# Mixers whose lanes begin at moments from a table, and weight pieces rounded five beats ahead of their product

## What is computed

```python
def first_block(...):                      # l = 0, 1
    h = h + 0.5 * swiglu(rmsnorm(h, ffn1_norm[l]), w_gate, w_up, w_down)   # d_ff = 2816
    z = rmsnorm(h, mix_norm[l]) @ w_in[l]
    y_mla, y_diff = mla_mixer(...), diff_mixer(...)       # causal attention over 256 rows
    y_pool = pool_mixer(...)                              # running means, then a small product
    branches = einsum('bsnc,ncd->bsnd', stack([y_mla, y_diff, y_pool]), w_branch[l])
    h = h + sum(sigmoid(z_gate) * branches) @ w_out[l]
    h = h + 0.5 * swiglu(rmsnorm(h, ffn2_norm[l]), ...)
return rmsnorm(h, final_norm)

def second_block(...):                     # l = 0, 1
    x = x + 0.5 * rms_norm(swiglu_2(rms_norm(x, ...), w_ffn1_in[l], w_ffn1_out[l]), ...)
    proj = rms_norm(x, ln_mix_pre[l]) @ w_in[l]
    y_attn = sliding_window_gqa(...)                      # 8 heads, window 128, sinks
    y_mlstm = mlstm_chunkwise(...)                        # chunks of 64
    y_rwkv = rwkv7_time_mix(...)                          # a recurrence, computed in chunks
    x = x + rms_norm(concat([y_attn, y_mlstm, y_rwkv]) @ w_out[l], ln_mix_post[l])
    x = x + 0.5 * rms_norm(swiglu_2(rms_norm(x, ...), ...), ...)
    gate = sigmoid(rms_norm(x, ln_ple_pre[l]) @ w_ple_gate[l])
    x = x + rms_norm(gate * (p[l] @ w_ple_proj[l]), ln_ple_post[l])
```

## Time and profile before

| | before |
|---|---|
| median of the runs | 2604.29 us |
| profiled execution, device time | 2605.03 us |
| its span (first to last instruction) | 2603.4 us |
| PE, matmul busy | 2420.7 us (93%) |
| PE, weight load busy | 2044.6 us (79%) |
| DVE busy | 1521.4 us (58%) |
| ACT busy | 1250.3 us (48%) |
| POOL busy | 54.2 us (2%) |
| casts (L260), 748 | 779.0 us |
| subtractions (L267), 748 | 905.4 us |

### The profile page before, as it was taken

One profiled execution on the slowest core, in us unless ns is written; L12 is line 12 of the kernel. 1 busy time (PEld: TensorE's weight loads), 2 busy tenths in 40 slices (PEclk: granted clock), 3 DMA queues, 4 the chain that ended last, 5 costly groups with the idle time before them and its releaser, 6 DMA issues.

```text
span 2603.4 us, 33966 instructions
## 1 busy us (share of the span) xinstructions
PE 2420.7 (93%) x13760; PEld 2044.6 (79%) x13760; DVE 1521.4 (58%) x2356; ACT 1250.3 (48%) x2095; POOL 54.2 (2%) x66
## 2 busy tenths in 40 slices
PE   7998889999999879999999978899988997989997
PEld 6888788888888878888878867678877886867885
DVE  4656576655655657665555566665555557466555
ACT  4445344544544535454454453544455444355444
POOL 0000000000000000000000000000000000000000
PEclk9999899999999989999999989889999998979999
DMA  6554234566566423456655633136645553214553
GB/s 237 195 184 145 81 114 135 180 187 187 178 188 188 149 86 116 136 178 186 187 167 187 188 128 99 58 111 196 187 151 177 186 189 96 89 49 163 190 187 111
DMA packets 110748, 400.12 MB, mean 154 GB/s; under 512 B 12288, under 2 KB 12672, under 8 KB 110336
## 3 DMA queue, kind: packets, MB, share of 16 engines
q1 hardware_dynamic: 110592, 397.96, 48.4%
HBM read 396.86 MB, written 1.05 MB: 153 GB/s over the span
## 4 chain that ended last, share of the span: by engine, by line
PE 79%; DVE 12%; ACT 5%; issue 2%; DMA 1%; POOL 0%; SPq 0%; ACTq 0%; DVEq 0%
PE ps L275 71%; DVE wlo L267 4%; ACT whi L260 2%; PE ps L561 2%; PE ps L1724 1%; DVE alo L417 1%; ACT ahi L394 1%; PE ps L1173 1%; PE ps L378 1%; DVE sm L1221 0%; DVE cv L2274 0%; PE ps L1129 0%; PE ps L1138 0%; ACT S L1190 0%; PE ps L1157 0%
## 5 line engine op out<-in xcount | busy, mean ns | idle before, releaser
L267 DVE TENSOR_TENSOR wlo<-raw,whi 128x1024 fp32r<-128x1024 f32 (+1 forms) x748 | 905.4, 1214 | 718.7 <-ACT whi L260 715.7
L260 ACT CAST whi<-raw 128x1024 fp32r<-128x1024 f32 (+1 forms) x748 | 779.0, 1046 | 663.7 <-PE ps L275 658.1
L275 PE MATMUL ps<-whi,ahi 128*128 128x512 f32 (+2 forms) x1632 | 655.9, 402 | 51.1 <-DVE alo L417 43.8
L275 PE MATMUL ps<-whi,alo 128*128 128x512 f32 (+2 forms) x1632 | 640.2, 392 | 0.0
L275 PE MATMUL ps<-wlo,ahi 128*128 128x512 f32 (+2 forms) x1632 | 639.1, 392 | 0.0
L275 PEld LDWEIGHTS ps<-whi,ahi 128*128 128x128 f32 x1632 | 312.0, 191 | 118.9 <-issue 43.9
L275 PEld LDWEIGHTS ps<-whi,alo 128*128 128x128 f32 x1632 | 311.7, 191 | 63.6
L275 PEld LDWEIGHTS ps<-wlo,ahi 128*128 128x128 f32 x1632 | 312.4, 191 | 58.1 <-issue 0.8
L275 PE MATMUL ps<-whi,yhi 128*128 128x512 f32 (+1 forms) x852 | 335.8, 394 | 2.0 <-DVE ylo L773 1.1
L275 PE MATMUL ps<-whi,ylo 128*128 128x512 f32 (+1 forms) x852 | 332.5, 390 | 0.0
L275 PE MATMUL ps<-wlo,yhi 128*128 128x512 f32 (+1 forms) x852 | 332.3, 390 | 0.0
(11 more groups left out here) (362 smaller groups left out, 2211.7 us busy)
## 6 DMA issues: line engine op xcount, KB each, us to landing
raw<-stream SPq DMA_DIRECT2D x718, 512.0 KB, 3.5
raw<-stream SPq DMA_DIRECT2D x16, 388.0 KB, 3.0
bcb<-bcs SPq DMA_DIRECT2D x9, 512.0 KB, 4.6
raw<-stream SPq DMA_DIRECT2D x8, 416.0 KB, 3.2
raw<-stream SPq DMA_DIRECT2D x4, 384.0 KB, 3.4
cst<-consts SPq DMA_DIRECT2D x1, 1260.0 KB, 6.0
msc<-misc SPq DMA_DIRECT2D x1, 1160.0 KB, 5.9
xs<-xin SPq DMA_DIRECT2D x2, 512.0 KB, 4.5
```

The source lines that it names most:

```text
L260: act.do.copy(whi[:, n % NSP, 0:w], raw[:, n % NRAW, 0:w]).then_inc(*rounded(n))
L267: dve.do.tensor_tensor(wlo[:, n % NSP, 0:w], raw[:, n % NRAW, 0:w], whi[:, n % NSP, 0:w].bitcast(F), ALU.subtract).then_inc(*rest(n))
L275: m = pe.do.matmul(o, a, b, start=(first and q == 0), stop=(last and q == n - 1))
```

## The change

Three things change, and no instruction is added or removed but for a few loads of ACT's function tables (35 in both programs; in L2106 two fewer, in L2242 two more).

- Each piece's rounding is placed by its product: `taken[n]` is PE's beat when it takes piece n, and the cast's beat is the later of the slot's beat and `taken[n]` less 5.0. The subtraction stands 0.5 behind. The DMA of piece n stands where piece n-4 is rounded.
- `freed` takes a distance from PE's own beat rather than a beat; `again` and `first_time` are gone.
- In the mixers, `timed` replaces the beats of every lane by those of a table `PLAN`, relative to `org(s)`. The lanes themselves and the order within each are the same. In `pe_unit` a wait for `"mask"` is one for `"T"`, which DVE sends one multiplication later.

```diff
+LEAD = 5.0
+
+PLAN = {
+    "mix1": {
...
+        "act_latent": (27.1, 31.6, 31.9, 36.1, 38.6, 41.7, 42.1, 42.6, 49.5, 49.5, 49.9, 49.9, 49.9),
...
+    "mix2": {
...
+        "dve_jobs2": (65.8, 67.3, 71.9, 73.4, 75.5, 78.3, 80.9, 83.9),
...
+        taken.append(pe.beat)
...
-    def freed(n, beat, by, *key):
-
-        free[n] = (beat, by.name, key)
+    def freed(n, d, by, *key):
+
+        free[n] = (pe.beat + d, by.name, key)
...
+    def round_beat(n):
+
+        return max(slot_beat(n - NSP), now_taken[n] - LEAD)
...
-            yield slot_beat(n - NRAW - NSP) if n >= NRAW else -2.0
+            yield round_beat(n - NRAW) if n >= NRAW else -2.0
...
     def act_weights():
         for n in range(len(pieces)):
-            yield slot_beat(n - NSP)
+            yield round_beat(n)
...
     def dve_weights():
         for n in range(len(pieces)):
-            yield slot_beat(n - NSP) + 0.5
+            yield round_beat(n) + 0.5
...
-    def first_time(s):
...
+    def timed(s, **lanes):
+
+        def one(name, lane):
+            plan = PLAN.get(PARTS[s][0], {}).get(name)
+            for k, beat in enumerate(lane):
+                yield org(s) + plan[k] if plan else beat
+        return [one(name, lane) for name, lane in lanes.items()]
...
-        def again(k, t):
-
-            return max(t, first_time(s + 1) + 1.36 * k - 2.6)
...
-                    freed(held[k][0], again(k, t + 0.68 * (h + k + 1)), dense, s, "held", k)
+                    freed(held[k][0], 0.68, dense, s, "held", k)
...
-                freed(n, t + GU * (r + 1), dense, s, *(("gu", q, 1) if r == 3 else ("g", q, r)))
+                freed(n, GU, dense, s, *(("gu", q, 1) if r == 3 else ("g", q, r)))
...
-            pe.wait_ge(rec_dve, s, 0, "mask", L64_)
+            pe.wait_ge(rec_dve, s, 0, "T")
...
             elif part == "mix1":
-                lanes += [tables_in(act, s), act_project1(s), act_latent(s, l), act_bias1(s), act_jobs1(s), act_back1(s), act_sums1(s),
-                          act_turn1(s, l), act_pool1(s), act_branch1(s)]
+                lanes += timed(s, tables_in=tables_in(act, s), act_project1=act_project1(s), act_latent=act_latent(s, l),
+                               act_bias1=act_bias1(s), act_jobs1=act_jobs1(s), act_back1=act_back1(s), act_sums1=act_sums1(s),
+                               act_turn1=act_turn1(s, l), act_pool1=act_pool1(s), act_branch1=act_branch1(s))
```

More of the change, by code:

```diff
@@ L220, in program @@
     stages = list(enumerate(PARTS))
-    free = {}
-    now_free, pieces = (known["free"], known["order"]) if known else (free, order)
+    free, taken = {}, []
+    now_free, now_taken, pieces = (known["free"], known["taken"], known["order"]) if known else (free, taken, order)
     def width(n):
@@ L510, in down @@
             m.then_inc(*dense(s, "d", j))
-            freed(n, t + GU, dense, s, "d", j)
+            freed(n, GU, dense, s, "d", j)
         t = step_beat(s, 0)
@@ L794, in pe_wide @@
             m.then_inc(*dense(s, *key, r, i))
-        freed(n, t + 2.9, dense, s, *key, r, 1)
+        freed(n, 2.2, dense, s, *key, r, 1)
     def region(at):
@@ L859, in pe_project1 @@
                 if i:
-                    freed(n, t + Z1 + 1.12 * (5 + r), dense, s, "z", r, 1)
+                    freed(n, 1.12, dense, s, "z", r, 1)
         for c in range(8):
@@ L960, in pe_latent @@
             m.then_inc(*front_pe(s, "v", i))
-        freed(n, t + 26, front_pe, s, "v", 1)
+        freed(n, 3.0, front_pe, s, "v", 1)
         for b in range(5):
@@ L2383, in pe_ple @@
             m.then_inc(*dense(s, "p", hf))
-            freed(n, t + 2.72 * (hf + 1), dense, s, "p", hf)
-        freed(n1, t + 5.44, dense, s, "p", 1)
+            freed(n, 2.72, dense, s, "p", hf)
+        freed(n1, 2.72, dense, s, "p", 1)
         def wait_y(k):
@@ L2443, in tensor_program @@
             elif part == "mix1":
-                lanes += [tables_in(pe, s), pe_project1(s, l), pe_latent(s, l), pe_scores1(s), pe_values1(s), pe_turn1(s, l),
-                          pe_pool1(s, l), pe_branch1(s, l), pe_out1(s, l)]
+                lanes += timed(s, tables_in=tables_in(pe, s), pe_project1=pe_project1(s, l), pe_latent=pe_latent(s, l),
+                               pe_scores1=pe_scores1(s), pe_values1=pe_values1(s), pe_turn1=pe_turn1(s, l), pe_pool1=pe_pool1(s,
+                               l), pe_branch1=pe_branch1(s, l), pe_out1=pe_out1(s, l))
             elif part == "mix2":
-                lanes += [pe_project2(s, l), pe_front2(s, l), pe_unit(s, 0), pe_unit(s, 1), pe_state(s), pe_group(s),
-                          pe_rope2(s), pe_scores2(s), pe_values2(s), pe_turn2(s), pe_memory(s, l), pe_out2(s, l)]
+                lanes += timed(s, pe_project2=pe_project2(s, l), pe_front2=pe_front2(s, l), pe_unit0=pe_unit(s, 0),
+                               pe_unit1=pe_unit(s, 1), pe_state=pe_state(s), pe_group=pe_group(s), pe_rope2=pe_rope2(s),
+                               pe_scores2=pe_scores2(s), pe_values2=pe_values2(s), pe_turn2=pe_turn2(s), pe_memory=pe_memory(s, l),
+                               pe_out2=pe_out2(s, l))
             else:
@@ L2513, in pool_program @@
             if part == "mix1":
-                lanes += [pool_latent(s), pool_sums1(s)]
+                lanes += timed(s, pool_latent=pool_latent(s), pool_sums1=pool_sums1(s))
             elif part == "mix2":
-                lanes += [pool_memory(s)]
+                lanes += timed(s, pool_memory=pool_memory(s))
             if part in POST and part != "final":
@@ L2550, in program @@
     sync_program()
-    return {"at": {name: x.at for name, x in signals.items()}, "free": free, "order": order}
+    return {"at": {name: x.at for name, x in signals.items()}, "free": free, "taken": taken, "order": order}
 def make_consts():
```

89 lines of the change are left out of this document (70 added, 19 removed), and 28 rows, old and new, of the table PLAN.

## The result

The changed kernel takes 2525.72 us (median of four runs, 2522.96 to 2525.82) against 2602.42 for the kernel before in the same comparison: a ratio of 0.9707, 95% interval 0.9686 to 0.9728, or some 76 us less.

A forecast was written before the change was run, and what follows sets the result against it. PE was taken as the bound, with gains only from its idle time in the mixers and the clock. The terms -22.1 - 3.6 - 4.0 + 1.0 gave -28.7 us, so 2575.6 us on the median, range 2560 to 2590.

The forecast's parts named there:

- part 5 of the sum: Inside the FFNs: roundings come later at no cost, hidden by PE's work, with 1.24 us left for piece 154.
- Part (1): In the four mixers: roundings leave the path, gaining 22.1 us of a ceiling of 44.7.
- Part (2): In mix1: the table's own moves shorten PE's wait for `pool_f`, 1.8 us each, 3.6 in all, bounds 0 and 14.4.
- Part (3): In mix2: fewer waits shorten the half-clock stretch, 2 us each, 4 in all, bounds 0 and 24.4.
- Rival A: Deeper: the waits taken away bring the clock back, -71.7 us, 2533 us; chance 0.15.
- Part (4): Between stages, around the norms: roundings move off and onto the path, net +1.0 us, bounds -6.6 and +7.6.
- D: Half: norms at stage borders cost +7.6 us and the share in the first part is 20%, 2590 us; chance 0.12.
- C: Nothing: work moved within a DVE-pressed stage comes back as another wait, 2605 us; chance 0.10.
- B: Slower: the cover in the FFNs fails and PE stalls 0.6 us a step, 2623 us; chance 0.13.

The follow-up runs named there:

- The rule alone: Changed kernel with the table PLAN emptied, so every lane has its old beats and only the new rounding rule stays: 2585.69 us, ratio 0.9936.
- that one lane: Changed kernel whose mix1 table keeps only `pe_values1`, PE's lane of the attention's second products, with mix2's table whole: 2554.86 us, ratio 0.9822.

## Why the prediction was wrong

**Direction and bound: right.** The gain was in the mixers, PE's work did not change, and the FFNs' insides kept their length: 16.79 us a step (part 5 of the sum). But the sizes were not as named: 38.5 and 32.0 us in the two mix1 where 7 to 9 each were to be seen, 2.8 and 4.8 in the two mix2 where 6 to 8 were.

**Part (1), roundings: right in sum by luck, wrong in place.** I took 22.1 of a ceiling of 44.7 us, by my shares some 9 in mix1 and 13 in mix2. The rule alone gave 9.4 + 12.6 in mix1, nearly the whole ceiling there (10.4 + 12.7), and -0.9 - 0.3 in mix2, 20.8 together. The share of 40% was one number for two stages that behave in opposite ways. The 3.5 us a mix2 that I called nearly certain did leave their stretch: no rounding stands in the chain between 1565 and 1605 us of the changed kernel, which corresponds, and from the 399th to the 441st product of weights the stage takes 46.4 us in place of 51.1, with the rule alone 48.6. But the rule alone had lost 2.8 us by the 399th, which I had not weighed.

**Part (2), the table: the step that failed.** I took a quarter of one wait, `pool_f`, 3.6 us in all with 14.4 as the bound. It is worth 29.1 and 19.4 us in mix1 (266.1 to 237.0 and 257.9 to 238.5) and 3.7 and 5.1 in mix2. Why: I looked through ACT's and DVE's programs for roundings, and took PE's own order as given. The wait I priced, `pool_f`, fell from 7.2 to 2.0 us. The ones I did not price fell more. What is left in the first mix1:

```profile
PE ps L369 <- DVE alo L511: 3.8, 1, 3.8
PE ps L1424 <- DVE pool_f L1446: 2.0, 2, 1.8
PE ps L1263 <- ACT PT L1291: 0.9, 3, 0.5
PE ps L1263 <- DVE PT L1332: 0.8, 1, 0.8
PE ps L1247 <- DVE ylo L863: 0.5, 1, 0.5
PE ps L369 <- DVE dk L1000: 0.2, 1, 0.2
```

Of the earlier trace rows, the wait for `zc` is gone. Of the waits before that follow, so are 7 of 8.7 us for `PT`, and those for `S`, `dv` and `o_dif` altogether:

```profile
PE ps L1173 <- ACT PT L1201: 4.4, 10, 0.7
PE ps L1173 <- DVE PT L1242: 4.3, 3, 1.7
PE ps L1157 <- DVE S L1231: 3.1, 4, 0.9
PE ps L275 <- ACT dv L900: 2.8, 1, 2.8
PE ps L761 <- DVE o_dif L1274: 2.2, 1, 2.2
```

The bound of the part should have been the whole of PE's idle time in mix1, 28 and 26 us, with the clock on top.

**Part (3), the clock: wrong stage.** I priced the long half-clock stretch in mix2, which stayed: from 1602 to 1633 us of the changed kernel the clock is 0.57.

```profile
1602.00:1633.00 31.00, 30.75 (x110) 23.03 (x110) 18.43 (x44) 17.26 (x36) 1.01 (x1) 0.57 0.21 68
```

Still in front of it is the stretch in which DVE has the chain, 24.90 of 27 us busy:

```profile
1575.00:1602.00 27.00, 23.22 (x120) 17.00 (x118) 24.90 (x50) 17.22 (x36) 0.00 (x0) 0.88 0.13 40
```

In mix1, whose half-clock stretches I left at nothing, 14.2 and 11.0 us of busy time went. Rival A's condition, that the waits go, was met in mix1; in mix2 it was not, where 23.8 and 24.9 of 29.8 us of idle time stayed, and the clock stayed at 0.85 and 0.87. The rule of the Trainium skill quoted in part (3) (TensorE: Matmul & The Clock Gate, section "HAM oscillation — how this bites in real kernels"), that waits between batches of matmuls bring the lower clock back, agrees in kind with the first mix1, where idle time fell from 32.4 to 8.1 us and the clock rose from 0.94 to 0.98.

**Part (4), between stages: near in sum.** Taken +1.0; the ten other stretches and the program's start together changed by -0.9, with 2.2 us lost behind the first ple as said. The subtraction that was to cost 1.2 us between the final norm and ffn1_2 does not show: that stretch is 0.6 us shorter.

**The rivals.** A's number, 2533, was nearest, for the wrong reason: its 24.4 us were mix2's clock. D and C did not come: the rule that moved work within a stage "comes back as another wait" is refuted in mix1 by the rule alone (22.0 us gained), and is what happened to the rule alone in mix2. B's mechanism is real but does not set in at 5.0 (the first ffn2 has one wait for `wlo`, of 0.3 us); at 4.5 it does.

## What to carry to other kernels

When a schedule moves several engines at once, bound its gain by all the idle time of the bounding engine in the stage plus the clock lost there, not by the sum of the moves that one can see; parts of a schedule priced one by one (16.7 and 10.5 us here) may be worth far more together (45.8). On the bounding engine look first for an operation placed directly behind the one that starts the helper it waits for, and put independent work between; that one lane was the largest single piece here. Place support work such as weight rounding late but not too late, and measure on both sides: 5.0 gave 2526 us, 4.5 gave 2584 and 7.0 gave 2575.

## What was unexpected of the hardware

A stall of 0.3 to 0.4 us of PE, repeated in every step, shows only in part as idle time and hardly in the view of waits (0.3 us listed for a whole FFN that is 4.1 us longer). PE's idle time rises from 0.4 to 1.6 us and its busy time from 188.8 to 191.7, at a clock of 1.00. Step time between two equal events is the view that finds it.
